# Gates and branches of the second block by token rows, another order of the modulation folds, an earlier start of the [hi|lo] products in the first feed-forward

## The chip, the cores and the metric

The kernel runs on one core of a Trainium2 chip. The metric is the device time of one execution in microseconds (us). Three runs of the kernel before took 802.23, 802.59 and 802.83 us, so the median is 802.59 us. The profile comes from one further execution, which took 802.78 us.

## The reference

The input is 256 tokens (S) of 1024 channels (D). Two transformer blocks follow each other; all numbers are float32.

- Block one: `mod = silu(c) @ w_ada + b_ada` gives six vectors of 1024: shift1, scale1, gate1, shift2, scale2, gate2. `h = rmsnorm(x) * (1 + scale1) + shift1`, `proj = h @ w_in`; a sliding-window attention and a differential attention; `merged = sigmoid(ga) * (out_a @ w_branch_swa) + sigmoid(gd) * (out_d @ w_branch_diff)`; `x = x + gate1 * (merged @ w_out)`; then `x = x + gate2 * conv_ffn(rmsnorm(x) * (1 + scale2) + shift2)`, a feed-forward of width 2816 with a causal convolution of width 3 and a GELU gate.
- Block two: `proj = rmsnorm(x) @ w_in_2` gives a short convolution, a block attention (moba), a cross attention to a memory, and three gates g1, g2, g3 of 1024 channels each. `merged = sigmoid(g1 + bg1) * (y_conv @ w_br_conv) + sigmoid(g2 + bg2) * (y_moba @ w_br_moba) + sigmoid(g3 + bg3) * (y_mem @ w_br_mem)`; `x = x + merged @ w_o`; then a feed-forward with SiLU.

The sigmoid is computed as `0.5 * (1 + tanh(z / 2))`; the factor 0.5 is applied when the merged sum is rounded.

## The kernel before, in words

**Products in two parts.** Every float32 operand is split into a rounded high part (`whi`, `hhi`) and the rest (`wlo`, `hlo`). A product is three matmuls: hi by hi, hi by lo, lo by hi. `hhi` and `hlo` are the halves of one tile, `h_two`.

**Units.** The weights arrive as 131 units of 128 x 2048 numbers (1 MB), in a ring of four raw slots (`raw`). SyncE loads a unit, ScalarE (ACT) rounds it (`round_unit`, line 516), VectorE (DVE) subtracts to get the low part (`split_low`, line 1100), TensorE (PE) multiplies. ACT and DVE work three units ahead (`AHEAD`). The order of the loads is the list `PLAN` (`build_plan`, line 50). Units are named by the first of their stage: `WIN1` (block one's input projection), `BR1` (4 units of branches), `WO1` (4 units of output projection), `FFN1` (33 units), then `WIN2` (26 units, the last 12 are the gates), `BR2` (6), `WO2` (4), `FFN2` (33).

**Four shapes of a unit's products.** (a) By channels (`channels`, `both_channels`, `abreast_half`): the weights are stationary, 256 token columns move, 48 matmuls of 256 columns. (b) Paired (`paired_channels`, `paired_half`): the high weights are stationary and `[hi|lo]` of the input move together as 512 columns, then the low weights with 256 columns: 16 matmuls of 512 and 16 of 256. The two halves of the PSUM bank have to be added afterwards: ACT copies one half out, DVE adds the other. (c) By token rows (`tall`, `branch_rows`): the input is stationary, 512 weight columns move, 24 matmuls of 512 columns; the result has tokens on the partitions. (d) Wide: the first four units of the first feed-forward (`wide_up`), whose moving operand has 256 tokens and two columns with the shift (`wide_hi`, `wide_lo`, 258 columns).

**Folds of the modulation.** `w_ada` is 24 pieces of 1 MB, each with the weights of two tiles of `mod`. `fold_ada` (line 1066) multiplies a piece with the spread silu(c) and sums it: two DVE instructions for a piece. From piece 10 on the pieces share the ring with the weights; `after` in `build_plan` says behind which unit a piece comes, and `split_low` of that unit is followed on DVE by the fold (`fold_after`). Pieces 12 to 15 make shift2, 16 to 19 scale2, 20 to 23 gate2.

**From block one's merge to its feed-forward.** DVE and ACT work in program order. In block one the merge is by rows (`merge`, k == 0, into `x_rows`); PE turns the merged rows to channels by eight 128 x 128 transposes for each half (`turn_merged`, line 2160), ACT rounds them, DVE makes the low part. Then DVE: gains, `shift_out` (a copy of shift2), the two shift columns of `wide_lo` (line 1450), and for u = 0 to 3 the new x of two channel tiles (line 1469), the low part of the scaled x (line 1174), the sums of squares (line 1122) and, at u = 1 and 2, `split_low` of units FFN1 and FFN1+1. PE starts `wide_up` when `wide_lo_ready` is set, takes channel tile after tile as `glo_ready` counts up, and after tile 5 sums the squares (`statistics("two")`, line 1889), which needs the squares of all eight tiles.

**Block two before.** Its gate units are paired: ACT copies the low half, DVE adds (line 1621), ACT takes the tanh with the bias as a scalar per channel. Its branches are by channels (`branch`), merged straight in channel layout (`mg`), so there is nothing to turn.

Of the kernel before, what the change touches and what calls it, by code (L numbers as in the profile page):

```python
# [18 lines left out]
ALU = mybir.AluOpType  # L19
# [119 lines left out]
MERGED_BANK = (2, 0)  # L139
# [3 lines left out]
FIRST_PAIRED = (4, 2)  # L143
PAIRED_A, PAIRED_G = ((0, 1), (0, 1)), ((2, 3), (2, 3))
# [7 lines left out]
def ring_landings(entry):  # L152
# [6 lines left out]
        WIN2: (0, 1), WIN2 + 2: (2, 7), WIN2 + 4: (0, 1), WIN2 + 6: (2, 7)}  # L159
# [7 lines left out]
def is_paired(w):  # L167
    return PAIRED_IN2 <= w < BR2


def unit_banks(w):
# [9 lines left out]
    for first, b in ((WO1, 4), (WO2, 6)):  # L181
        if first <= w < first + 4:
            return ((b + w - first) % 8,)
# [5 lines left out]
def build_evacuations():  # L189
# [7 lines left out]
    for w in [*range(FFN1), *range(WIN2, FFN2)]:  # L197
        if w == WIN2:
            last_in = {}
        if is_paired(w):  # L200
# [5 lines left out]
            if kind == "cc":  # L206
                done[w] = done[w, 1]
            else:
                emptied_by("act" if kind == "g" else "dve", w)
            continue  # L210
        on_dve = BR1 <= w < FFN1 or BR2 <= w < FFN2
# [26 lines left out]
def two_blocks(nc, t, out):  # L238
    ctx = ExitStack()
    with ctx:  # L240
# [52 lines left out]
        gate, _ = place("gate", [P, 24, S], F32, at=scratch_at)  # L293
        gate_rows, _ = place("gate_rows", [P, 2, NT, D], F32, at=scratch_at)
# [24 lines left out]
        def low_tile(k, i):  # L319
            kind = IN2[k][0]  # L320
            if kind == "g":
                return gate[:, 2 * (k - 14) + i, :]
# [4 lines left out]
        A_LOW = ("low_copied", "a_low1")  # L327

# [16 lines left out]
        half_bg = small[:, 64:88]  # L345
# [50 lines left out]
        def _(sp):  # L396
# [8 lines left out]

            def load_beside(a):
# [15 lines left out]
            for r, (kind, n) in enumerate(PLAN):  # L422
                if r == 3:
                    sp.dma_start(vec[:, FIRST_VECTORS:NV], t["vectors"][:, FIRST_VECTORS:NV]).then_inc(sem("vec_landed"), 16)
                if (kind, n) == ("ada", 4):
                    sp.dma_start(lam_in[:, :, :].rearrange("p a b -> p (a b)"), t["diff_lambda"])\
                        .then_inc(sem("lam_landed"), 16)
                if r == 2:
                    sp.dma_start(xt[:, :, :], t["x_rows"].rearrange("(a p) b -> p a b", p=P)).then_inc(sem("xt_landed"), 16)
                if (kind, n) == ("w", WIN1 + 13):  # L430
                    sp.dma_start(x[:, :, :].rearrange("p a b -> p (a b)"), t["x"]).then_inc(sem("x_landed"), 16)
                if (kind, n) == ("w", WIN1 + 9):
                    sp.wait_ge(sem("hlo_ready"), KT)
                    sp.dma_start(memt[:, :, :], t["mem_rows"].rearrange("(a p) b -> p a b", p=P))\
                        .then_inc(sem("memt_landed"), 16)
# [78 lines left out]
        def _(act):  # L514
# [230 lines left out]
            for s in range(18):  # L745
# [43 lines left out]
                if s == 13:  # L789
                    act.wait_ge(sem("memt_landed"), 16)  # L790
# [26 lines left out]
            def merge_and_project(b0, nbr, o0, k, name, gain):  # L817

                for u in range(1, 2 * nbr):
                    if k and u == nbr:  # L820
                        round_merged(k, 0)
                    if u < 2 * nbr - 1:
                        round_unit(b0 + u + AHEAD)
                if k == 0:
                    round_turned(0)
                    round_unit(o0 + AHEAD - 1)
                    round_turned(1)
                else:
                    round_merged(k, 1)
                    round_unit(o0 + AHEAD - 1)  # L830
                for u in range(4):
# [3 lines left out]
                    if k == 0 and u == 0:  # L835
# [12 lines left out]
            def round_turned(half):  # L848
                act.wait_ge(sem("turned_in"), 3 + half)
                for i in range(2):  # L850
                    c = 4 * half + 2 * i
                    copy(hhi[:, c:c + 2, :], pair(ps[:, MERGED_BANK[half] + i, :]), scale=0.5).then_inc(sem("mghi_ready"), 1)

            def round_merged(k, half):
                for i in range(2):
                    act.wait_ge(sem("merged"), 4 * k + 2 * half + i + 1)
                    c = 4 * half + 2 * i
                    copy(hhi[:, c:c + 2, :], mg[:, c:c + 2, :], scale=0.5).then_inc(sem("mghi_ready"), 1)
# [7 lines left out]
            def ffn(f):  # L866
# [45 lines left out]
                def slot(c, kind, j, it=0):  # L912
# [18 lines left out]
                    if f == 1 and c == 2:  # L931
                        act.wait_ge(sem("turned_in"), 7)
# [34 lines left out]
            for s in range(27):  # L967
                if s == 2:
                    root("memk", tokens=eps_mem)
                if s >= 1:  # L970
# [23 lines left out]
                    else:  # L994
# [42 lines left out]
        def _(dve):  # L1037
# [191 lines left out]
            V.tensor_scalar(half_bg, col("b_gate_2", n=24), 0.5, None, ALU.mult)  # L1229
# [24 lines left out]
            dve.wait_ge(sem("lam_landed"), 16)  # L1254
# [129 lines left out]
            def merge(w, b, nbr, k, by_bank=False):  # L1384
# [3 lines left out]
                for i, bank in enumerate(unit_banks(w)):  # L1388
                    if by_bank and i == 1:
                        dve.wait_ge(gemm_done, w + 1)  # L1390
                    c = 4 * half + 2 * i
                    if k == 0:
                        g = gate_rows[:, r, i, 512 * half:512 * half + 512]
                        dst, sums, term = x_rows[:, i, 512 * half:512 * half + 512], ps[:, bank, :], probs[:, i, 0:512]
                    else:
                        g = gate[:, KT * r + c:KT * r + c + 2, :]
                        dst, sums, term = mg[:, c:c + 2, :], pair(ps[:, bank, :]), pair(probs[:, i, 0:512])
# [18 lines left out]
            def low_merged(k, half):  # L1416
                for i in range(2):
                    dve.wait_ge(sem("mghi_ready"), 4 * k + 2 * half + i + 1)
                    c = slice(4 * half + 2 * i, 4 * half + 2 * i + 2)
                    src = mg[:, c, :] if k else pair(ps[:, MERGED_BANK[half] + i, :])  # L1420
                    V.scalar_tensor_tensor(out=hlo[:, c, :], in0=src, scalar=0.5, in1=f32(hhi[:, c, :]),
                                           op0=ALU.mult, op1=ALU.subtract).then_inc(sem("mglo_ready"), 1)

            def merge_all(b0, nbr, o0, k):
                for u in range(1, 2 * nbr):
                    merge(b0 + u - 1, u - 1, nbr, k)
                    if k and u % nbr == 0:
                        low_merged(k, 0)
                    if u < 2 * nbr - 1:
                        split_low(b0 + u + AHEAD)  # L1430
                if k == 0:
                    low_merged(k, 0)
                merge(b0 + 2 * nbr - 1, 2 * nbr - 1, nbr, k, by_bank=True)
                if k == 0:
                    split_low(o0 + AHEAD - 1)
                    low_merged(k, 1)
                else:
                    low_merged(k, 1)
                    split_low(o0 + AHEAD - 1)
# [3 lines left out]
            def two_gain(c):  # L1443
# [8 lines left out]
            dve.wait_ge(sem("x_landed"), 16)  # L1452
            dve.wait_ge(raw_done, ada_folded(2))
            for u in range(4):
# [167 lines left out]

            def mix_norm():
# [16 lines left out]
            for s in range(27):  # L1640
# [112 lines left out]
        def _(pe):  # L1753
# [379 lines left out]
            def branch(w, tile0, waits, last=False):  # L2133
                begin(w)
                for s_, n in waits:
                    pe.wait_ge(s_, n)
                for i in range(4):
# [278 lines left out]
```

## Time and profile before

| | us |
|---|---|
| median of three runs | 802.59 |
| the profiled execution | 802.78 |
| its span, first to last instruction | 801.0 |
| PE busy | 791.0 (99%) |
| DVE busy | 638.2 (80%) |
| ACT busy | 454.3 (57%) |
| POOL busy | 32.1 (4%) |

The span is 1.8 us shorter than the execution. PE's granted clock was 1.00 over the whole span. A busy PE is modelled: a matmul's shown duration overlaps with the next one's, so the pace of PE is read from the distance of the starts, not from the durations.

### The profile page before, as it was taken

The numbers are of one execution on the slowest core, as the hardware profiler recorded it, in microseconds if no ns is written. First come the engines' busy times: TensorE is split into PE (matmuls) and PEld (weight loads), VectorE is DVE, ScalarE is ACT, GpSimd is POOL, SyncE is SP. The second block draws the span as 40 slices with busy tenths as digits, with TensorE's granted clock in tenths as the row PEclk, the third lists the DMA queues.
The fourth block names the chain that finished last, engine by engine and source line by source line (L and its number), as shares of the span: only waits on it lengthen the run. The fifth ranks groups of instructions, "written<-read, shape, count | busy, mean of one in ns | idle before, by whom it ended". The sixth has DMA issues, their size and how long they took to land.

```text
span 801.0 us, 12246 instructions
## 1 busy us (share of the span) xinstructions
PE 791.0 (99%) x4888; PEld 704.6 (88%) x4888; DVE 638.2 (80%) x955; ACT 454.3 (57%) x649; POOL 32.1 (4%) x32
## 2 busy tenths in 40 slices
PE   7999999999999999999999999999999999999998
PEld 7899778889999888888888888889999988888887
DVE  4998999997888987776887898755777777777775
ACT  7848677637556345454876657775436644545451
POOL 2000000000000000000000000000000121111210
DMA  9996948964536866554354544444444555455411
GB/s 359 420 420 248 355 165 304 381 253 158 215 137 236 317 254 215 203 209 160 136 185 160 203 158 158 158 158 158 158 169 153 210 209 207 158 209 212 170 41 53
DMA packets 25480, 168.86 MB, mean 211 GB/s; under 512 B 2896, under 2 KB 3408, under 8 KB 5840
## 3 DMA queue, kind: packets, MB, share of 16 engines
q1 hardware_dynamic: 25280, 168.08, 56.7%
q8 instruction: 39, 0.64, 0.3%
q14 instruction: 17, 0.14, 0.1%
q10 hardware_dynamic: 144, 0.01, 0.0%
HBM read 167.03 MB, written 1.05 MB: 210 GB/s over the span
## 4 chain that ended last, share of the span: by engine, by line
PE 88%; DVE 7%; DMA 2%; ACT 2%; issue 1%; SPq 0%; ACTq 0%
PE ps L1761 46%; PE ps L1796 23%; PE ps L1803 12%; DVE wlo L1100 2%; PE ps L1857 2%; DVE raw L1066 1%; PE ps L2037 1%; DMA raw<-in_w_mem_kv 1%; ACT whi L516 1%; PE ps L2070 1%; PE ps L2008 1%; PE ps L2009 1%; DMA raw<-in_branches 1%; DVE wlo L1095 1%; DVE side_x L1066 0%
## 5 line engine op out<-in xcount | busy, mean ns | idle before, releaser
L1100 DVE TENSOR_TENSOR wlo<-raw,whi 128x2048 fp32r<-128x2048 f32 (+1 forms) x130 | 287.1, 2215 | 62.6 <-ACT whi L516 58.3
L516 ACT ACTIVATE whi<-raw 128x2048 fp32r<-128x2048 f32 (+2 forms) x144 | 251.0, 1756 | 82.2 <-PE ps L1796 42.6
L1796 PE MATMUL ps<-h_two,whi 128*128 128x512 f32 x512 | 123.8, 392 | 0.0
L1796 PEld LDWEIGHTS ps<-h_two,whi 128*128 128x128 f32 x512 | 94.1, 188 | 18.3
L1761 PE MATMUL ps<-h_two,whi 128*128 128x256 f32 x544 | 99.3, 285 | 1.8 <-DVE wlo L1095 1.6
L1761 PEld LDWEIGHTS ps<-h_two,whi 128*128 128x128 f32 x544 | 84.7, 192 | 2.8 <-DVE wlo L1095 1.8
L1761 PE MATMUL ps<-h_two,wlo 128*128 128x256 f32 x272 | 76.9, 283 | 0.0
L1761 PE MATMUL ps<-whi,fhi 128*128 128x512 f32 (+1 forms) x178 | 69.1, 388 | 0.0
L1761 PE MATMUL ps<-whi,flo 128*128 128x512 f32 (+1 forms) x178 | 68.9, 387 | 0.0
L1761 PE MATMUL ps<-wlo,fhi 128*128 128x512 f32 (+1 forms) x178 | 68.8, 387 | 0.0
L1796 PE MATMUL ps<-g_two,whi 128*128 128x512 f32 x288 | 68.4, 390 | 0.0
L1803 PEld LDWEIGHTS ps<-h_two,wlo 128*128 128x128 f32 x512 | 65.4, 191 | 3.5 <-issue 1.0
L1803 PE MATMUL ps<-h_two,wlo 128*128 128x256 f32 x512 | 67.6, 285 | 0.0
L1796 PEld LDWEIGHTS ps<-g_two,whi 128*128 128x128 f32 x288 | 53.5, 188 | 10.7
L499 POOL TENSOR_TENSOR fg<-fg,spread_r 128x512 f32<-128x512 f32 x11 | 27.3, 2480 | 743.1 <-ACT fg L516 743.1
L516 ACT ACTIVATE fhi<-fp 128x512 fp32r<-128x512 f32 x22 | 13.9, 632 | 68.7 <-DVE fp L1567 50.1
L1761 PEld LDWEIGHTS ps<-h_two,wlo 128*128 128x128 f32 x272 | 52.1, 192 | 0.0
L1761 PE MATMUL ps<-whi,h_two 128*128 128x512 f32 x160 | 50.2, 395 | 0.0
L1761 PE MATMUL ps<-whi,g_two 128*128 128x512 f32 x128 | 40.1, 395 | 0.0
L1761 PEld LDWEIGHTS ps<-whi,fhi 128*128 128x128 f32 x178 | 33.4, 188 | 7.1 <-issue 0.4
L1761 PEld LDWEIGHTS ps<-wlo,fhi 128*128 128x128 f32 x178 | 33.4, 188 | 6.8
L1761 PEld LDWEIGHTS ps<-whi,flo 128*128 128x128 f32 x178 | 33.4, 188 | 6.6
(278 smaller groups left out, 1424.1 us busy)
## 6 DMA issues: line engine op xcount, KB each, us to landing
raw<-in_w_up SPq DMA_DIRECT2D x44, 1024.0 KB, 4.8
raw<-in_w_in SPq DMA_DIRECT2D x43, 1024.0 KB, 4.8
raw<-in_w_down SPq DMA_DIRECT2D x22, 1024.0 KB, 4.8
raw<-in_w_ada SPq DMA_DIRECT2D x14, 1024.0 KB, 5.2
raw<-in_branches SPq DMA_DIRECT2D x10, 1024.0 KB, 4.8
raw<-in_w_out SPq DMA_DIRECT2D x4, 1024.0 KB, 6.9
raw<-in_w_o SPq DMA_DIRECT2D x4, 1024.0 KB, 4.7
raw<-in_w_mem_kv SPq DMA_DIRECT2D x3, 1024.0 KB, 11.2
```

Of the source, the lines that this page charges most:

```text
L499: nc.gpsimd.tensor_tensor(fg[:, b, :].rearrange("p (a b) -> p a b", a=2), fg[:, b, :].rearrange("p (a b) -> p a b", a=2), spread_r[:, :].u ...
L516: return nc.scalar.activation(dst, src, func, **kw)
L1066: ins = V.tensor_tensor_reduce(out=piece, in0=piece, in1=cs[:, :], scale=1.0, scalar=col("b_ada", c), op0=ALU.mult, op1=ALU.add, accum_out ...
L1095: V.tensor_tensor(wlo[:, w % SPLIT, 0:c], raw[:, slot, 0:c], f32(whi[:, w % SPLIT, 0:c]), ALU.subtract).then_inc(sem("half_lo"), 1)
L1100: V.tensor_tensor(wlo[:, w % SPLIT, c:UNIT], raw[:, slot, c:UNIT], f32(whi[:, w % SPLIT, c:UNIT]), ALU.subtract).then_inc(raw_done, 1)
L1761: ins = mm(out_, l, r, start=start and i == 0, stop=stop and i == 2, **kw)
L1796: ins = mm(ps[:, b, :], wt(whi, w, kt, P * i, P, 256), two[:, :, kt, :], start=start and kt == 0, stop=stop and kt == KT - 1, skip_group_c ...
L1803: ins = mm(ps[:, b, S:2 * S], wt(wlo, w, kt, P * i, P, 256), two[:, 0, kt, :], start=start and kt == 0, stop=stop and kt == KT - 1, skip_g ...
L1857: ins = mm(ps[:, b, S * i:S * i + S], wt(w_, w, kt, P * i, P, 256), a_[:, kt, :], start=kt == 0 and i == 0 and n == 0, stop=kt == KT - 1 a ...
L2008: mm(ps[:, b, 0:first], q[:, 0:P], k[:, 0:first], start=True, stop=True)
L2009: ins = mm(ps[:, b, first:first + 256], q[:, P:2 * P], k[:, 0:256], start=True, stop=True)
L2037: ins = nc.tensor.transpose(ps[:, b, dst:dst + P], probs[:, m, src:src + P], ident[:, :])
```

## The change

1. The 12 gate units of block two go by rows, two units sharing two PSUM banks. The gate bias comes as rows: three loads of 1 MB (`load_bias`) into the gate tile, DVE adds PSUM to it (`add_bias`, two instructions of 128 x 512 for two units), ACT takes the tanh (two of 128 x 512). The copies of low halves go, and the small `half_bg`.
2. The six branch units of block two go by rows (`branch_rows`), merged in rows, turned by `turn_merged(1, 0)` and `(1, 1)`, and the first two units of `WO2` are taken half by half as in block one. Unit `WO2+2` is paired and its result added in two steps.
3. The folds: pieces 16 to 19 come before 12 to 14, nothing stands behind `BR1+3`, piece 15 comes behind unit `FFN1`, pieces 20 to 23 behind `FFN1+15, 18, 21, 24`. `shift_out` is copied at u = 1, `wide_lo`'s shift columns are made at u = 2 of the loop over `WO1`.
4. The first feed-forward's products are paired from column pair 3 on, before from 4 (two units). The bank pairs change parity.

```diff
-    after = {WIN1 + at: (a,) for a, at in enumerate((9, 12, 13, 14, 15, 16, 17, 18, 19, 20), 10)}
-    after[WIN1 + 10] = (9,)
-    after.update({FFN1 + at: (a,) for a, at in enumerate((9, 12, 15, 18), 20)})
+    behind = {9: 10, 10: 9, 12: 11, 13: 16, 14: 17, 15: 18, 16: 19, 17: 12, 18: 13, 19: 14, FFN1 - WIN1: 15}
+    after = {WIN1 + at: (a,) for at, a in behind.items()}
+    after.update({FFN1 + at: (a,) for a, at in enumerate((15, 18, 21, 24), 20)})
...
-MERGED_BANK = (2, 0)
+MERGED_BANK = ((2, 0), (6, 4))
+PAIRED_OUT2 = 2
...
-FIRST_PAIRED = (4, 2)
-PAIRED_A, PAIRED_G = ((0, 1), (0, 1)), ((2, 3), (2, 3))
+FIRST_PAIRED = (3, 2)
+PAIRED_A, PAIRED_G = ((2, 3), (0, 1)), ((0, 1), (2, 3))
...
+        **{WIN2 + 14 + 2 * p: ((2, 6), (0, 1))[p % 2] for p in range(6)}}
...
+                if (kind, n) == ("w", WIN2 + 15):
+                    sp.wait_ge(sem("x3_ready"), 1)
+                    load_bias(0)
+                if (kind, n) == ("w", WIN2 + 23):
+                    sp.wait_ge(sem("yclo_ready"), 2)
+                    load_bias(1)
+                    load_bias(2)
...
             def gate_tanh(k):
-                if k < 0 or IN2[k][0] != "g":
+                if k < 14 or k % 2 == 0:
                     return
-                w, g = WIN2 + k, 2 * (k - 14)
-                for i in range(2):
-                    act.wait_ge(emptied["dve"], EVACUATED[w, i][1])
-                    ins = copy(gate[:, g + i, :], gate[:, g + i, :], ACT.Tanh, scale=0.5, bias=half_bg[:, g + i:g + i + 1])
-                ins.then_inc(emptied["act"], 1)
+                r, columns = gate_pair(k)
+                for tt in range(NT):
+                    act.wait_ge(emptied["dve"], EVACUATED[WIN2 + k - 1 + tt][1])
+                    g = gate_rows[:, r, tt, columns]
+                    copy(g, g, ACT.Tanh, scale=0.5)
...
-            dve.wait_ge(raw_done, ada_folded(3))
-            V.tensor_copy(shift_out, mod[:, 24:32]).then_inc(sem("shift_ready"), 1)
-            dve.wait_ge(sem("wide_hi_ready"), 1)
-            V.tensor_tensor(wide_lo[:, :, S:WIDE], mod[:, 24:32].unsqueeze(2).to_broadcast([P, KT, 2]),
-                            f32(wide_hi[:, :, S:WIDE]), ALU.subtract).then_inc(sem("wide_lo_ready"), 1)
...
                 if u in (1, 2):
                     sum_squares("two", SQUARES["two"], mg, u - 1)
                     split_low(w + AHEAD)
+                if u == 1:
+                    dve.wait_ge(raw_done, ada_folded(3))
+                    V.tensor_copy(shift_out, mod[:, 24:32]).then_inc(sem("shift_ready"), 1)
+                if u == 2:
+                    dve.wait_ge(sem("wide_hi_ready"), 1)
+                    V.tensor_tensor(wide_lo[:, :, S:WIDE], mod[:, 24:32].unsqueeze(2).to_broadcast([P, KT, 2]),
+                                    f32(wide_hi[:, :, S:WIDE]), ALU.subtract).then_inc(sem("wide_lo_ready"), 1)
...
+            def add_bias(k):
+                r, columns = gate_pair(k)
+                dve.wait_ge(gemm_done, WIN2 + k + 1)
+                dve.wait_ge(sem(BIAS_LANDED[r]), 32)
+                for tt in range(NT):
+                    g = gate_rows[:, r, tt, columns]
+                    V.tensor_tensor(g, g, ps[:, unit_banks(WIN2 + k)[tt], :], ALU.add).then_inc(emptied["dve"], 1)
...
+                xs, banks = x[:, 2 * u:2 * u + 2, :], unit_banks(w)
+                if u == PAIRED_OUT2:
+                    link(V.tensor_tensor(xs, xs, half_of(banks, 0), ALU.add))
+                sums = half_of(banks, 1) if u == PAIRED_OUT2 else pair(ps[:, banks[0], :])
+                V.tensor_tensor(xs, xs, sums, ALU.add).then_inc(sem("x5_ready"), 1)
...
             def project_merged(o0, k):
-                if k == 0:
-                    begin(o0)
-                    ...
+                begin(o0)
+                abreast_half(o0, k, 0, 0)
+                turn_merged(k, 1)
+                begin(o0 + 1)
+                abreast_half(o0, k, 1, 0)
+                for u in range(2):
+                    abreast_half(o0, k, u, 1)
+                for u in (2, 3):
                     begin(o0 + u)
-                    if u == 0:
-                        both_channels(o0, (sem("mglo_ready"), 4 * k, 2))
+                    if k and u == PAIRED_OUT2:
+                        paired_channels(o0 + u, unit_banks(o0 + u), h_two, False)
                         continue
...
-                branch(BR2 + u, 4 * r, [[(sem("yclo_ready"), 2)], [(sem("ylo_ready"), 8)], [(sem("ylo_ready"), 10)]][r], last=u == 5)
+                if u == 4:
+                    turn_merged(1, 0)
+                branch_rows(BR2 + u, 4 * r, [[(sem("yclo_ready"), 2)], [(sem("ylo_ready"), 8)], [(sem("ylo_ready"), 10)]][r], u == 5)
```

## Rows read from the trace of the kernel before

**Rows 1.** The page: busy time, share of the span and instructions of each engine.
```profile
PE 791.0 (99%) x4888; PEld 704.6 (88%) x4888; DVE 638.2 (80%) x955; ACT 454.3 (57%) x649; POOL 32.1 (4%) x32
```
**Rows 2.** Waits of PE: who waited for whom, us in total, times, longest.
```profile
PE ps L1944 <- DVE small L1207: 4.2, 1, 4.2
PE ps L1761 <- DVE wlo L1095: 1.8, 2, 1.6
```
**Rows 3.** Table by stretches: length, busy us of each engine, clock, DMA; BR1, then BR2.
```profile
153.33:176.12 22.79, 22.79 (x106) 18.77 (x104) 21.16 (x26) 9.74 (x8) 0.00 (x0) 1.00 0.88 331
...
555.08:589.63 34.55, 34.55 (x289) 34.55 (x288) 25.62 (x27) 12.71 (x12) 0.00 (x0) 1.00 0.51 183
```
**Rows 4.** Timeline of PE, gate units: start, duration, operation, count.
```profile
542.10 3.82 PE L1796 MATMUL ps<-h_two,whi 128*128 128x512 f32 x16
545.76 2.08 PE L1803 MATMUL ps<-h_two,wlo 128*128 128x256 f32 x16
547.67 3.82 PE L1796 MATMUL ps<-h_two,whi 128*128 128x512 f32 x16
```
**Rows 5.** Timeline of PE: where units start in WO1 and FFN1.
```profile
194.26 0.40 PE L1761 MATMUL ps<-h_two,whi 128*128 128x256 f32 x2
...
200.02 0.28 PE L1761 MATMUL ps<-wide_hi,whi 128*128 128x258 f32 x1
...
204.37 0.95 PE L1889 MATMUL ps<-mean_d,proj 128*128 128x1 f32 x8
...
241.14 0.40 PE L1761 MATMUL ps<-whi,fhi 128*128 128x512 f32 x1
...
246.60 0.40 PE L1761 MATMUL ps<-h_two,whi 128*128 128x256 f32 x2
```
**Rows 6.** The chain that ended last, in order of time: the two turns.
```profile
169.81 0.99 PE ps L2160 x8
...
179.16 0.87 PE ps L2160 x8
```
**Rows 7.** Timeline of DVE during WO1.
```profile
188.71 0.88 DVE L1469 SCALAR_TENSOR_TENSOR x<-ps,small,x 128x256 f32<-128x256 f32 x2
...
192.14 2.29 DVE L1100 TENSOR_TENSOR wlo<-raw,whi 128x2048 fp32r<-128x2048 f32 x1
194.47 0.88 DVE L1469 SCALAR_TENSOR_TENSOR x<-ps,small,x 128x256 f32<-128x256 f32 x2
...
197.64 2.29 DVE L1100 TENSOR_TENSOR wlo<-raw,whi 128x2048 fp32r<-128x2048 f32 x1
199.85 0.48 DVE L1469 SCALAR_TENSOR_TENSOR x<-ps,small,x 128x256 f32<-128x256 f32 x1
```
**Rows 8.** Timeline of DVE: a fold's first instruction and what follows the fold.
```profile
160.99 1.28 DVE L1066 CUSTOM_DVE_ANT_0 raw<-raw,cs,vec 128x1024 f32<-128x1024 f32 x1
...
163.40 1.28 DVE L1399 SCALAR_TENSOR_TENSOR x_rows<-gate_rows,ps 128x512 f32<-128x512 f32 x2
```
**Rows 9.** Timeline of DVE during WO1: `wide_lo`'s shift columns, then the first x.
```profile
185.84 0.18 DVE L1450 TENSOR_TENSOR wide_lo<-small,wide_hi 128x16 fp32r<-128x16 f32 x1 [0.28 <-ACT wide_hi L516]
186.31 0.88 DVE L1469 SCALAR_TENSOR_TENSOR x<-ps,small,x 128x256 f32<-128x256 f32 x2 [0.29 <-issue]
```
**Rows 10.** Timeline of ACT: the square of tile 7.
```profile
203.49 0.40 ACT L516 ACTIVATE proj<-x 128x256 f32<-128x256 f32 x1
```
**Rows 11.** Timeline of DVE: the product of pair 2 in the first feed-forward.
```profile
252.83 0.68 DVE L1569 TENSOR_TENSOR fp<-fg,ps 128x512 f32<-128x512 f32 x1
```
**Rows 12.** The gate tile: count, duration in ns min/median/max, first and last start.
```profile
L1621 DVE TENSOR_TENSOR gate<-gate,ps x24: 410/414/422, 483.7 to 556.0; 128x256 f32<-128x256 f32 x24
```
**Rows 13.** Timeline of DVE in BR2 and WO2: first of a merge, then an x.
```profile
572.55 0.69 DVE L1403 SCALAR_TENSOR_TENSOR probs<-gate,ps 128x512 f32<-128x512 f32 x1 [0.57 <-PE ps L1761]
...
612.94 0.69 DVE L1724 TENSOR_TENSOR x<-x,ps 128x512 f32<-128x512 f32 x1 [0.62 <-PE ps L1761]
```
**Rows 14.** The page: DMA issues, KB each, median us from issue to landing.
```profile
raw<-in_w_in SPq DMA_DIRECT2D x43, 1024.0 KB, 4.8
```

More of the change, by code:

```diff
@@ L167, in is_paired @@
 def is_paired(w):
-    return PAIRED_IN2 <= w < BR2
+    return PAIRED_IN2 <= w < WIN2 + 14
 def unit_banks(w):
@@ L180, in unit_banks @@
             return (b, b + 1)
-    for first, b in ((WO1, 4), (WO2, 6)):
-        if first <= w < first + 4:
-            return ((b + w - first) % 8,)
+    if WO1 <= w < WO1 + 4:
+        return (4 + w - WO1,)
+    if WO2 <= w < WO2 + 4:
+        return ((6,), (7,), (0, 1), (3,))[w - WO2]
     if w >= WIN1 + FIRST and w < WIN2:
@@ L208, in build_evacuations @@
             else:
-                emptied_by("act" if kind == "g" else "dve", w)
+                emptied_by("dve", w)
             continue
-        on_dve = BR1 <= w < FFN1 or BR2 <= w < FFN2
+        on_dve = BR1 <= w < FFN1 or WIN2 + 14 <= w < FFN2
         emptied_by("x1" if WO1 <= w < FFN1 else "x5" if WO2 <= w < FFN2 else "dve" if on_dve else "act", w)
@@ L292, in two_blocks @@
         side_proj, _ = place("side_proj", [P, 2, D], F32, at=proj_at + 8 * S * 4)
-        gate, _ = place("gate", [P, 24, S], F32, at=scratch_at)
-        gate_rows, _ = place("gate_rows", [P, 2, NT, D], F32, at=scratch_at)
+        gate_rows, _ = place("gate_rows", [P, 3, NT, D], F32, at=scratch_at)
         tmp, _ = place("tmp", [P, KT, S], F32, at=scratch_at + 16 * S * 4)
@@ L819, in merge_and_project @@
                 for u in range(1, 2 * nbr):
-                    if k and u == nbr:
-                        round_merged(k, 0)
                     if u < 2 * nbr - 1:
                         round_unit(b0 + u + AHEAD)
-                if k == 0:
[L825 to L830, printed above, removed]
+                round_turned(k, 0)
+                round_unit(o0 + AHEAD - 1)
+                round_turned(k, 1)
                 for u in range(4):
@@ L846, in merge_and_project, with round_turned @@
                         square(x, mg, u, sem(name))
-            def round_turned(half):
-                act.wait_ge(sem("turned_in"), 3 + half)
+            def round_turned(k, half):
+                act.wait_ge(sem("turned_in"), (3, 7)[k] + half)
                 for i in range(2):
                     c = 4 * half + 2 * i
[L852 to L858, printed above, removed]
+                    copy(hhi[:, c:c + 2, :], pair(ps[:, MERGED_BANK[k][half] + i, :]), scale=0.5).then_inc(sem("mghi_ready"), 1)
             merge_and_project(BR1, 2, WO1, 0, "x1_ready", lambda c: gs2[:, c:c + 1])
@@ L1390, in merge @@
                         dve.wait_ge(gemm_done, w + 1)
[L1391 to L1397, printed above, removed]
+                    g = gate_rows[:, r, i, 512 * half:512 * half + 512]
+                    dst, sums, term = x_rows[:, i, 512 * half:512 * half + 512], ps[:, bank, :], probs[:, i, 0:512]
                     if r == 0:
@@ L1419, in low_merged @@
                     c = slice(4 * half + 2 * i, 4 * half + 2 * i + 2)
-                    src = mg[:, c, :] if k else pair(ps[:, MERGED_BANK[half] + i, :])
-                    V.scalar_tensor_tensor(out=hlo[:, c, :], in0=src, scalar=0.5, in1=f32(hhi[:, c, :]),
+                    V.scalar_tensor_tensor(out=hlo[:, c, :], in0=pair(ps[:, MERGED_BANK[k][half] + i, :]), scalar=0.5, in1=f32(hhi[:, c, :]),
                                            op0=ALU.mult, op1=ALU.subtract).then_inc(sem("mglo_ready"), 1)
@@ L1426, in merge_all @@
                     merge(b0 + u - 1, u - 1, nbr, k)
-                    if k and u % nbr == 0:
-                        low_merged(k, 0)
                     if u < 2 * nbr - 1:
                         split_low(b0 + u + AHEAD)
-                if k == 0:
-                    low_merged(k, 0)
+                low_merged(k, 0)
                 merge(b0 + 2 * nbr - 1, 2 * nbr - 1, nbr, k, by_bank=True)
[L1434 to L1439, printed above, removed]
+                split_low(o0 + AHEAD - 1)
+                low_merged(k, 1)
                 split_low(o0 + AHEAD)
@@ L1646, in _ @@
                     add_halves(s - 1)
+                if s > 14 and s % 2 == 0:
+                    add_bias(s - 1)
                 if s not in ITEMS2:
@@ L2131, in _ @@
                 slot(w, ITEMS1, s, halves)
[L2133 to L2137, printed above, removed]
-                    channels(w, i, 512, yhi[:, tile0:tile0 + 4, :], ylo[:, tile0:tile0 + 4, :], 4, last=i == 3,
-                             signal=sem("first_bank_done") if last and i == 1 else None)
             def branch_rows(w, tile0, waits, last):
```

56 lines of the change are left out of this document (25 added, 31 removed), and 2 rows, old and new, of the table VECTORS.

## The prediction

> **What bounds the kernel now.** I read the page's first part, PE's own list of waits, the table by stretches and the timeline of PE. PE is busy 99% of the span and DVE 80% [rows 1]. PE waits only in the start-up: 4.2 us for the spread of c and 1.8 us for a low part [rows 2]; none of its waits from 50 us on, but for a few tenths in block one's attention, is in that list. The reader is to see a stream of matmuls without holes, so the time is the number of matmuls by their pace, and the pace is the distance of starts. Whatever leaves this stream is gained in full, and whatever holds PE in a place where it was never held is lost in full. So there are two sums: the pace of the forms that change, and a look at each place where DVE or ACT works differently, asking whether PE comes to wait. The clock is 1.00 in both stretches of [rows 3], so a nanosecond is the same all along.
>
> **Paces.** By channels (48 matmuls of 256): 194.26 to 200.02, 5.76 us a unit [rows 5]; BR2's six units give the same, 34.55 / 6 = 5.76 [rows 3]. Paired: 542.10 to 547.67, 5.57 us [rows 4]. By rows (24 of 512): BR1's four units and one turn take 22.79 us [rows 3], the turn 0.99 [rows 6], so (22.79 - 0.99) / 4 = 5.45 us; the down unit from 241.14 to 246.60, the same shape, took 5.46 [rows 5].
>
> **Part 1, gate units by rows.** 12 x (5.57 - 5.45) = 1.4 us off PE. DVE's work shrinks: before, 24 adds of 414 ns [rows 12], after, 12 of about 0.69 (the 128 x 512 add from PSUM, [rows 13]), so 9.9 becomes 8.3 us; ACT loses 24 copies and keeps as many tanh columns. Only even steps have `add_bias`, and attention items sit on odd ones, so the attention's chain gets shorter. A bank pair comes back two units after `add_bias` was due, over 5 us of cover. The bias loads are 3 MB more on SP's queue. Two waits of SP precede them: `x3_ready` and `yclo_ready`; both are set by DVE in the step whose `split_low` releases the neighbouring weight load anyway, and what is queued behind (a unit needed three steps, some 16 us, later) takes 4.8 us to land [rows 14]. I count them at nothing; if the three transfers went strictly one behind another it would be 3 x 4.8 = 14.4 us, still under 16. Bounds 0 to 2 us, taken 0.
>
> **Part 2, branches by rows.** 34.55 - 6 x 5.45 = 1.85 us off PE. `WO2+2` paired: 5.76 - 5.57 = 0.2 off. Two turns are added, priced by block one's, 0.99 and 0.87 [rows 6]: 1.86 us on. Do PE's new waits bite? A merge is four operations of 0.69 [rows 13], 2.9 us with what lies between them, a split 2.3 [rows 7]; together 5.2 in a unit that shrinks from 5.76 to 5.45. Before, DVE still waited 0.57 us for PE ahead of a merge [rows 13], so about 0.25 is left. The turn of half 0 comes one whole unit after its merge is due, the turn of half 1 a half unit (2.9 us) after the last matmul of BR2, against 0.2 + two operations (1.4) for the last merge. Block one does exactly this, there with folds between [rows 8], and its turns cost 0.99 and 0.87 and no wait [rows 2, 6]. I take no wait; bounds 0 to 1 us. The paired `WO2+2` costs DVE one more add (0.7), which ends in the 0.62 us that DVE waited before the last x [rows 13]; PE needs what follows only for its tile 6, over 4 us into FFN2. Nothing.
>
> The trace prices the forms at 5.76 and 5.45 [rows 3]. The Trainium skill ("TensorE: Matmul & The Clock Gate", Back-to-back issue gap) has, for a single matmul, N/2.4 + 2.5 ns, so 109 ns at 256 and 216 at 512: by it a unit is 5.24 by channels and 5.18 by rows, and parts 1, 2 and 4 would bring 0.7 us of PE together in place of 3.8; the sum would end 3.1 us higher. The rows time this very pair of forms, so the measurement decides. The same page (Part 4: PE-mode transpose) has about 275 ns for a transpose in a kernel; 16 of them would be 4.4 us, while the rows have 1.86, since here they follow each other closer than their durations.
>
> **Part 4, pair 3 of the first feed-forward.** Two units, 2 x (5.76 - 5.57) = 0.4 off. The new condition is that g(3) starts only when product 2 is done, before product 1 was enough. Product 2 was ready at 253.5 [rows 11], and g(3) will want to start at 246.60 + 5.57 = 252.2 [rows 5]: it would be 1.3 late, but the fold that stood in that step (2.4 us, below) moves to a later one, so 251.1. Nothing; 1.3 us if I am wrong on that.
>
> **Part 3, the folds.** A fold is 163.40 - 160.99 = 2.41 us of DVE [rows 8]. Taken from `BR1+3`, where PE was not waiting for DVE, it brings PE nothing. It is put behind `split_low(FFN1)`, in the u = 1 step of WO1, and DVE runs in order. Here is the loop before [rows 7]: u = 1 from 188.71, split of FFN1 from 192.14, x of u = 2 at 194.47, split from 197.64, x of tile 6 at 199.85. The inserted: 2.41 fold, about 0.25 for its wait and the copy of shift2. Off it come 0.1 of DVE slack before 194.47 and about 0.4, since the copy and the shift columns that delayed the first x to 186.31 [rows 9] are gone and ACT's rounding starts as much earlier. Net +2.15: x of u = 2 at 196.6, the second split ends at 199.85 + 2.15 = 202.0, and only then come the shift columns (0.18), so `wide_lo_ready` at 202.2. PE wants it at 200.02 [rows 5]. **PE waits 2.2 us** where it never did. A second chain through the same delay: PE sums the squares 4.35 us into the unit (204.37 - 200.02), and the square of tile 7 ended at 203.9 [rows 5, 10]; it moves by 2.3 to 206.2, PE's place to 202.2 + 4.35 = 206.55. The two overlap, and only the first is paid. If DVE's cover is better than I think, the wait is 0; if worse, 2.6. Taken 2.2.
>
> The fold's later place in the feed-forward (pieces 20 to 23) falls in steps of the same make as those which held one before; nothing. `half_bg` leaves the start-up, 0.1 at most.
>
> **The sum.** Off: 1.4 + 1.85 + 0.2 + 0.4 + 0.1 = 3.95. On: 1.86 + 2.2 = 4.06. Net +0.1 us: 801.0 + 0.1 of span plus 1.8 outside is 802.9 against the profiled 802.78. The median shown is 0.2 below that execution, so I forecast 802.7. A measurement of this kernel tells 0.2%, 1.6 us, from no change; this is the same.
>
> **Rivals.**
> - *The fold is covered.* PE does not wait at FFN1: 802.7 - 2.2 = 800.5, faster by 0.26%. For it: DVE was only 80% busy, and it loses a fold before WO1 [rows 1, 8]. Against: in WO1 it idled only 0.1 us between the split of 192.14 and the next x, and one wait inside an in-order queue can't be caught up from before. Chance 0.19.
> - *Both waits of the first wide unit add (slower).* PE waits for the shift columns, and then for the squares at its tile 6, because ACT, which now sits in its u = 2 step behind `shift_ready`, passes the delay on a second time. It decides from the point where tile 7's square comes more than 4.35 us after PE's start; if it came late by the whole chain again, 2.3 more: 805.0, slower by 0.3%. Against: my 206.2 stands before 206.55, if by 0.35 only, and before the change the same chain was ready at 203.9 for 204.37. With a late turn in block two (1 us) instead, the time is 803.7, which is still the same. Chance 0.08.
> - *The bias or the banks arrive late.* DVE stands in `add_bias`, splits behind it are late and PE waits; 2 us, 804.7. A unit's cover of 16 us speaks against. Chance 0.03.
> - *Rows bring no pace in block two.* The change does not do what it says: 1.4 + 1.85 missing, 806.0. Against: [rows 3] of block one. Chance 0.02.
>
> **Numbers.** Forecast 0.68. Faster 0.21: the covered case, and 0.02 of the forecast's for a half-covered wait that passes 801.0. Slower (above 804.2) 0.13, the three last rivals. Same 0.66. The likeliest case's own range is 802.0 to 803.7 (wait of 1.8 to 2.6, turns up to 1 late). The range for 8 in 10 takes in the covered case: 800.4 to 803.9.
>
> **What would show it.** Right: in the timeline of PE a hole of about 2 us ahead of the first matmul of 258 columns, released by DVE's line for the shift columns of `wide_lo`; two folding instructions between a split and an x in DVE's WO1; gate and branch units 5.45 us apart; two turns of eight transposes in block two at 0.9 each with no idle time; DVE's list with 12 adds on the gate rows. Wrong: no hole there and everything else as said gives 800.5; a hole in front of the turns, of `WO2`, of g(3) or at the sums of squares gives more than 802.7.

## The result, and the profile after

The kernel before takes 802.65 us (802.23 to 803.87, 12 runs), the changed one 804.18 us (802.82 to 806.03, 12 runs): a ratio of 1.0018, 95% interval 1.001 to 1.0026. I forecast 802.7 and a range up to 803.9, so the time is outside. The profiled execution of the changed kernel took 804.81 us, with a span of 802.7 and a mean granted clock (the share of TensorE's full speed) of 0.998; that of before 802.78, 801.0 and 1.000.

The page's first part after, for [rows 1]. PE is busy 1.5 us less, the half clock told of below included, and DVE as long as before:
```profile
PE 789.5 (98%) x4616; PEld 691.5 (86%) x4616; DVE 639.0 (80%) x945; ACT 446.1 (56%) x614; POOL 32.1 (4%) x32
```
PE's waits after, for [rows 2]: who waited for whom, us in total, times, longest.
```profile
PE ps L1948 <- DVE small L1209: 4.4, 1, 4.4
PE ps L1765 <- DVE wlo L1097: 3.0, 3, 1.6
PE ps L1765 <- DVE wlo L1102: 2.0, 1, 2.0
PE ps L1960 <- DVE wlo L1219: 0.7, 2, 0.5
```
The third is new, one wait of 2.0 us; the others lie in the start-up, as in [rows 2]. The timeline of DVE in WO1 shows where it comes from, against [rows 7, 9]:
```profile
191.83 2.29 DVE L1102 TENSOR_TENSOR wlo<-raw,whi 128x2048 fp32r<-128x2048 f32 x1
194.04 1.28 DVE L1068 CUSTOM_DVE_ANT_0 raw<-raw,cs,vec 128x1024 f32<-128x1024 f32 x1
...
195.24 1.28 DVE L1068 CUSTOM_DVE_ANT_0 raw<-raw,cs,vec 128x1024 f32<-128x1024 f32 x1
...
196.57 0.17 DVE L1466 COPY small<-small 128x8 f32<-128x8 f32 x1
196.65 0.87 DVE L1452 SCALAR_TENSOR_TENSOR x<-ps,small,x 128x256 f32<-128x256 f32 x2
...
199.81 2.29 DVE L1102 TENSOR_TENSOR wlo<-raw,whi 128x2048 fp32r<-128x2048 f32 x1
202.02 0.17 DVE L1469 TENSOR_TENSOR wide_lo<-small,wide_hi 128x16 fp32r<-128x16 f32 x1
```
The fold stands between the split of FFN1's weights and the x of u = 2; everything behind it is 2.2 us later, and the shift columns of `wide_lo` are the last of it. The timeline of PE over the same place is the one to read line by line; the first number is the start, so the distance from line to line is the pace:
```profile
199.96 0.28 PE L1765 MATMUL ps<-h_two,wlo 128*128 128x256 f32 x1
202.29 0.36 PE L1765 MATMUL ps<-wide_hi,whi 128*128 128x258 f32 x1 [2.05 <-DVE wlo L1102]
202.48 0.28 PE L1765 MATMUL ps<-wide_lo,whi 128*128 128x258 f32 x1
202.60 0.28 PE L1765 MATMUL ps<-wide_hi,wlo 128*128 128x258 f32 x1
202.72 0.28 PE L1765 MATMUL ps<-wide_hi,whi 128*128 128x258 f32 x1
202.84 0.35 PE L1765 MATMUL ps<-wide_lo,whi 128*128 128x258 f32 x1
202.99 0.42 PE L1765 MATMUL ps<-wide_hi,wlo 128*128 128x258 f32 x1
203.21 0.42 PE L1765 MATMUL ps<-wide_hi,whi 128*128 128x258 f32 x1
203.42 0.42 PE L1765 MATMUL ps<-wide_lo,whi 128*128 128x258 f32 x1
...
206.22 0.34 PE L1765 MATMUL ps<-wide_hi,wlo 128*128 128x258 f32 x1
206.39 0.28 PE L1765 MATMUL ps<-wide_hi,whi 128*128 128x258 f32 x1
206.51 0.29 PE L1765 MATMUL ps<-wide_lo,whi 128*128 128x258 f32 x1
...
208.21 0.95 PE L1893 MATMUL ps<-mean_d,proj 128*128 128x1 f32 x8
```
The hole is where the prediction put it: PE starts at 202.29 instead of 200.02 [rows 5]. What follows wasn't in the prediction. The first matmuls behind the hole come 0.12 us apart, then, from 202.99 on, the same ones come 0.215 apart, until 206.2. The table by stretches says why (length; busy us of PE, PEld, DVE, ACT and POOL; granted clock; DMA share; GB/s):
```profile
199.00:203.00 4.00, 1.95 (x17) 1.78 (x16) 3.51 (x5) 2.17 (x2) 0.00 (x0) 0.99 0.42 176
203.00:206.20 3.20, 3.20 (x17) 3.20 (x16) 2.40 (x6) 1.30 (x5) 0.00 (x0) 0.50 0.89 325
206.20:208.00 1.80, 1.80 (x17) 1.80 (x16) 0.16 (x1) 1.75 (x1) 0.00 (x0) 0.97 0.01 5
```
The granted clock is 0.50 for 3.2 us, the lower of the two levels, 1.2 GHz. PE had been at work at 1.00, since 50 us with waits of a few tenths at most, then it was idle for 2.2 us, then back at work for 0.6 us at 1.00 before the clock fell. The price by the starts: 18 distances from 202.84 to 206.51 are 3.67 us, and at 0.12 would be 2.16, so 1.5 us. PE counts as busy all along: neither the list of waits nor the busy share shows this loss, only the clock column and the distance of starts do.

Block two, from the timeline of DVE:
```profile
568.32 0.69 DVE L1399 SCALAR_TENSOR_TENSOR probs<-gate_rows,ps 128x512 f32<-128x512 f32 x1 [1.14 <-PE ps L1765]
...
573.76 0.69 DVE L1399 SCALAR_TENSOR_TENSOR probs<-gate_rows,ps 128x512 f32<-128x512 f32 x1 [0.25 <-PE ps L1765]
...
579.20 1.28 DVE L1395 SCALAR_TENSOR_TENSOR x_rows<-gate_rows,ps 128x512 f32<-128x512 f32 x2 [0.25 <-PE ps L1765]
```
Each line follows the end of a branch unit: they are 5.44 us apart, against 5.76 by channels [rows 3, 5], and DVE waits 0.25 us for PE, the slack that the prediction left it. The chain that ended last, in block two, has the turns:
```profile
569.86 9.30 PE ps L1765 x41
579.16 0.87 PE ps L2156 x8
580.03 13.77 PE ps L1765 x72
593.80 0.87 PE ps L2156 x8
```
and the gate tile's list (count, duration in ns min/median/max, first and last start) has 12 adds where [rows 12] had 24:
```profile
L1620 DVE TENSOR_TENSOR gate_rows<-gate_rows,ps x12: 672/680/687, 493.8 to 558.0; 128x512 f32<-128x512 f32 x12
```

### The profile page after: what moved, and what is told of

Same layout as the page of the kernel before. It is cut to its first block, busy times and chain, and to the rows that moved or that the text cites. A ratio compares the mean times of both kernels' runs of the same rounds, so it can differ in the third digit from the quotient of the medians.

```text
span 802.7 us, 11659 instructions
## 1 busy us (share of the span) xinstructions
PE 789.5 (98%) x4616; PEld 691.5 (86%) x4616; DVE 639.0 (80%) x945; ACT 446.1 (56%) x614; POOL 32.1 (4%) x32
## 4 chain that ended last, share of the span: by engine, by line
PE 90%; DVE 6%; ACT 2%; DMA 1%; issue 1%; SPq 0%; DVEq 0%; ACTq 0%
PE ps L1765 54%; PE ps L1800 19%; PE ps L1807 10%; DVE wlo L1102 2%; PE ps L1861 1%; PE ps L2041 1%; DMA raw<-in_w_mem_kv 1%; PE ps L2074 1%; ACT whi L530 1%; PE ps L2012 1%; PE ps L2013 1%; DVE wlo L1097 1%; DVE raw L1068 1%; DVE side_x L1068 0%; PE ps L2156 0%
## 5 line engine op out<-in xcount | busy, mean ns | idle before, releaser
L1765 PE MATMUL ps<-whi,h_two 128*128 128x512 f32 x352 | 110.7, 396 | 0.0
L1765 PE MATMUL ps<-h_two,whi 128*128 128x256 f32 x480 | 87.9, 285 | 1.7 <-DVE wlo L1097 1.6
L1800 PE MATMUL ps<-h_two,whi 128*128 128x512 f32 x368 | 88.0, 390 | 0.0
L1800 PEld LDWEIGHTS ps<-h_two,whi 128*128 128x128 f32 x368 | 68.0, 188 | 13.5
L1765 PEld LDWEIGHTS ps<-h_two,whi 128*128 128x128 f32 x480 | 74.7, 191 | 2.7 <-DVE wlo L1097 1.8
L1765 PEld LDWEIGHTS ps<-whi,h_two 128*128 128x128 f32 x352 | 64.9, 188 | 13.3 <-issue 0.7
L1765 PE MATMUL ps<-wlo,h_two 128*128 128x512 f32 x176 | 68.7, 390 | 0.0
L1765 PE MATMUL ps<-h_two,wlo 128*128 128x256 f32 x240 | 67.8, 283 | 0.0
L1807 PEld LDWEIGHTS ps<-h_two,wlo 128*128 128x128 f32 x368 | 46.3, 191 | 1.8 <-issue 0.7
L1807 PE MATMUL ps<-h_two,wlo 128*128 128x256 f32 x368 | 47.2, 283 | 0.0
L1765 PEld LDWEIGHTS ps<-h_two,wlo 128*128 128x128 f32 x240 | 46.0, 191 | 0.0
L1765 PE MATMUL ps<-whi,yhi 128*128 128x512 f32 (+1 forms) x112 | 40.5, 362 | 0.7 <-DVE wlo L1097 0.7
L1765 PE MATMUL ps<-wlo,yhi 128*128 128x512 f32 (+1 forms) x112 | 40.2, 359 | 0.0
```

Of the source, the lines that this page charges most:

```text
L1765: ins = mm(out_, l, r, start=start and i == 0, stop=stop and i == 2, **kw)
L1800: ins = mm(ps[:, b, :], wt(whi, w, kt, P * i, P, 256), two[:, :, kt, :], start=start and kt == 0, stop=stop and kt == KT - 1, skip_group_c ...
L1807: ins = mm(ps[:, b, S:2 * S], wt(wlo, w, kt, P * i, P, 256), two[:, 0, kt, :], start=start and kt == 0, stop=stop and kt == KT - 1, skip_g ...
```

## The experiments

**The fold and its companions put back.** Everything of the change stays but Part 3's hold on WO1:
```
-    behind = {..., 19: 14, FFN1 - WIN1: 15}
+    behind = {..., 19: 14, 20: 15}
```
with the copy of shift2, the shift columns of `wide_lo` and ACT's rounding of them ahead of the WO1 loop again.

> The changed kernel with piece 15 behind BR1+3 again (not behind FFN1), and the shift copy and the shift columns of wide_lo ahead of the loop over WO1 again. Rows, turns, pair 3, the order of the other pieces and the later pieces 20 to 23 stay. Theory A (the wait at the first wide unit costs its 2.2 us, and 1.65 us more because the granted clock is halved for 3.3 us after it): no hole before the first matmul of 258 columns, clock 1.00 throughout, 804.2 - 3.85 = 800.3 us. Theory B (the wait costs only its length; the remaining 1.5 us over the forecast come from the bias loads, the turns or the new rows): 804.2 - 2.2 = 802.0 us. Theory C (nothing of it is in part 3): 804.2 us.

Measured: 800.67 us (800.28 to 801.24, 11 runs) against 802.62 for before; 0.9975, interval 0.9967 to 0.9984. The clock is 1.000 in all 11. There is no hole at FFN1, as the timeline of PE shows:
```profile
199.75 0.28 PE L1763 MATMUL ps<-h_two,wlo 128*128 128x256 f32 x1
199.87 0.28 PE L1763 MATMUL ps<-wide_hi,whi 128*128 128x258 f32 x1
200.00 0.28 PE L1763 MATMUL ps<-wide_lo,whi 128*128 128x258 f32 x1
```
Parts 1, 2 and 4 bring 1.95 us together. It is faster than both kernels, by 0.25% than before; the next version is within 0.05 us of it. In the span they bring 2.2 us (798.6 against 800.8, medians), and the time outside the span takes 0.2 back: its median is 1.95 to 2.05 us in every version with the rows of block two, and 1.8 in before, in Part 3 alone and in pair 3 alone.

**Only the fold put back**, the copy and the shift columns in their new steps:

> The changed kernel with only piece 15 put back behind BR1+3; the shift copy stays at u = 1 and the shift columns at u = 2. Theory A: the inserted fold is the cause; the second split of the loop ends at 199.8 again, the columns at 200.0 to 200.1, so PE waits 0.1 to 0.3 us and the clock stays: 800.3 to 800.7 us. Rival: the columns' place behind the second split is what holds PE, by about 2 us, and lowers the clock: 804 us.

Measured: 800.72 us (800.24 to 801.37, 11 runs), 0.9978 (0.997 to 0.9987), all at clock 1.000. In the trace PE's last matmul of WO1 starts at 199.34 and its first wide one at 199.55, 0.1 us later than the pace of 0.12 would have it. So the later place of the small operations costs nothing that shows in the time; the 2.4 us of fold in that step is what makes the hole.

**Part 3 alone**, on the kernel before:
```
...
-    after[WIN1 + 10] = (9,)
...
+    behind = {9: 10, 10: 9, ..., 19: 14, FFN1 - WIN1: 15}
...
```
with pieces 20 to 23 and the fold's companions moved as in the change.

> The kernel before with part 3 alone: the new order of the pieces, piece 15 behind FFN1, 20 to 23 later, the shift steps at u = 1 and u = 2. No rows in block two, no pair 3. Theory A: a hole of 2.2 us at 200.0 and a clock drop behind it, 802.65 + 3.85 = 806.5 us. Theory B: 804.9 us. Theory C: 802.7 us.

Measured: 804.76 us (804.43 to 805.4, 8 runs), 1.0028 (1.0018 to 1.0039). The hole is there, but all eight executions have clock 1.000, and the cost is 804.76 - 802.62 = 2.14 us, the hole's length and no more. What I expected with the clock's fall, 806.5, didn't come, so with this run alone the clock was in doubt.

**The changed kernel again**, on another chip:

> The changed kernel once more, beside the two that hold PE, on one chip. Refined theory A: PE's hole of 2.2 us is in every execution, the halved clock behind it only in some (9 of 12 before). Executions whose mean clock is 1.00 take about 802.9 us, those at 0.998 about 804.2; the median depends on how many fall. Rival: the time over the forecast is in executions of either clock alike.

Measured: 803.05 us (802.35 to 804.41, 11 runs), 1.0009 (1.0 to 1.0018). Here 4 executions have a clock of 0.998 and take 803.92 to 804.41; the seven at 1.000 have a median of 802.79. The profiled one was of the latter. Its stretches at FFN1:
```profile
199.00:202.00 3.00, 0.95 (x9) 0.78 (x8) 2.96 (x4) 1.38 (x1) 0.00 (x0) 1.00 0.42 178
202.00:204.00 2.00, 2.00 (x17) 2.00 (x18) 1.39 (x4) 0.82 (x2) 0.00 (x0) 1.00 0.57 156
204.00:206.00 2.00, 2.00 (x19) 2.00 (x18) 1.34 (x4) 1.07 (x3) 0.00 (x0) 1.00 0.87 369
```
PE is busy 0.95 of the 3.00 us from 199, so the hole is the same, and no half clock follows it. So the same program has it in some executions and not in others.

**The shift columns one step earlier**, the fold left where the change has it:
```
-                if u == 2:
+                if u == 1:
                     dve.wait_ge(sem("wide_hi_ready"), 1)
```

> The changed kernel with the fold where it is, but DVE makes the shift columns of wide_lo at u = 1, right behind the copy of shift2. Theory A with its second chain: PE starts the first wide unit at 200.0, and then waits about 2 us at its sums of squares, which need tile 7's square at about 206.5 where PE comes by at 204.4; the hole has moved, its size and what follows it not: 803.5 to 804.7 us. Rival (the shift columns alone held PE): 800.3 to 801 us.

Measured: 803.87 us (802.65 to 806.76, 12 runs), 1.0017 (1.0007 to 1.0027). PE's first wide matmul no longer waits (200.73, then 200.85), and the delay comes out at the sums of the squares:
```profile
206.10 0.61 PE L1893 MATMUL ps<-mean_d,proj 128*128 128x1 f32 x4 [0.75 <-DVE proj L1124]
207.34 0.61 PE L1893 MATMUL ps<-mean_d,proj 128*128 128x1 f32 x4 [0.63 <-ACT proj L530]
```
From the first wide matmul to the transposes of `rstd` it is 209.49 - 200.85 = 8.64 us, against 206.54 - 199.87 = 6.67 with the fold put back: 2.0 us, the same price in another place. That is the second chain of the prediction: it overlapped with the first, and once the first wait was gone it was paid instead. Moving the needed columns out of the fold's way doesn't help; the delay sits in DVE's queue and reaches PE by the next edge. The profiled execution took 803.76 us; about 1 us of that is older than the hole (its first wide matmul starts at 200.85 against 199.87, behind longer waits in the start-up), while the median of the five executions at clock 1.000 is 802.75, again 800.7 and 2.1. The other seven fell: four have a clock of 0.998 (median 804.10) and three 0.996 (805.18). So in this version, whose wait comes in two pieces of 0.75 and 0.63 us, executions fell as well; none of the fallen was profiled, so where in them the clock was low isn't shown.

**A hole without any change of DVE's order.** On the version with everything put back, GpSimd clears a spare 128 x 512 tile when WO1's matmuls are done, and PE waits for it before the first wide matmul, on a count of a semaphore that exists:
```
...
+            pool.wait_ge(gemm_done, FFN1)
+            for i in range(3):
+                nc.gpsimd.memset(spare[:, :], 0.0).then_inc(sem("const_made"), 1)
+                pool.wait_ge(sem("const_made"), MADE_ALL + i + 1)
...
                     pe.wait_ge(sem("wide_lo_ready"), 1)
+                    if c == 0:
+                        pe.wait_ge(sem("const_made"), MADE_ALL + 3)
```

> The kernel with fold and code back (800.67 us), and PE alone held ahead of the first matmul of 258 columns: GpSimd clears a spare tile three times once WO1 is done, and PE waits for that. DVE and ACT keep their work and order. Theory A: a hole of 2 to 2.4 us costs its length in every execution, 802.9, and where the clock falls behind it 1.3 to 1.7 more, to 804.4; if the hole by itself is what lowers the clock, some executions show 0.998. Rival (the clock falls only with the fold of the changed kernel on DVE): all executions at 1.00 and 802.9 us.

Measured: 803.96 us (802.19 to 805.26, 11 runs), 1.0013 (1.0004 to 1.0022). Four executions at clock 1.000 have a median of 802.69, which is 800.67 and the hole of 2.03; seven at 0.998 have 804.38. The profiled one is of these: the three clears on POOL, then PE's first wide matmul, then the stretches:
```profile
200.04 1.69 POOL L521 MEMSET spare<- 128x512 f32 x3 [181.33 <-PE ps L1768]
201.95 0.36 PE L1768 MATMUL ps<-wide_hi,whi 128*128 128x258 f32 x1 [2.03 <-DVE wide_lo L1181]
...
202.00:204.00 2.00, 2.00 (x11) 2.00 (x12) 1.26 (x3) 1.19 (x3) 0.00 (x0) 0.61 0.88 369
204.00:206.00 2.00, 2.00 (x12) 2.00 (x11) 0.00 (x0) 1.43 (x1) 0.00 (x0) 0.54 0.00 0
206.00:208.00 2.00, 2.00 (x19) 2.00 (x19) 0.00 (x0) 0.00 (x0) 0.00 (x0) 1.00 0.00 0
```
The profile puts PE's wait down to DVE's L1181, but that instruction had ended at 201.12; the last clear ended at 201.73, 0.2 us before PE's start. An idle PE, with DVE's order as in the version without a hole, is enough to bring the half clock in some executions.

**The same with six clears:**

> The same with six clears: a hole of 4 to 4.4 us. Theory A: a longer hole lowers the clock in more executions, or for longer: all below 1.00, 800.7 + 4.2 + 1.6 or more = 806.5 us and above. Rival (clock falls by chance and not by the hole): 804.9 us at 1.00 in most.

Measured: 807.15 us (806.37 to 807.78, 5 runs), 1.0054 (1.004 to 1.0068); all five below 1.000, four at 0.996. PE stands still from 200.1 to 204.04, and the stretches are:
```profile
202.00:204.00 2.00, 0.00 (x0) 0.00 (x0) 1.39 (x4) 0.85 (x3) 1.66 (x4) 0.79 1.01 422
204.00:206.00 2.00, 1.96 (x9) 1.99 (x10) 0.18 (x1) 1.77 (x1) 0.00 (x0) 0.50 0.02 8
206.00:208.00 2.00, 2.00 (x11) 2.00 (x11) 0.00 (x0) 0.00 (x0) 0.00 (x0) 0.50 0.00 0
208.00:210.00 2.00, 2.00 (x12) 2.00 (x11) 0.00 (x0) 0.00 (x0) 0.00 (x0) 0.50 0.00 0
210.00:212.00 2.00, 2.00 (x19) 2.00 (x19) 0.00 (x0) 0.00 (x0) 0.00 (x0) 1.00 0.00 0
```
Here the clock falls while PE still stands (0.79 in the first line), stays low for 6 us of matmuls and costs about 2.7: 807.15 less 800.67 and the hole of 3.8.

**Pair 3 alone**, on the kernel before, with the folds where they were:
```
-FIRST_PAIRED = (4, 2)
+FIRST_PAIRED = (3, 2)
```
and the bank pairs swapped as in the change.

> The kernel before with pair 3 of the first feed-forward paired and the banks' parity changed, the folds where they were. The forecast said that g(3) would then wait 1.3 us for product 2 (253.5 against 252.2), and that the later folds are what spares it. If so: PE's list shows about 1.3 us on DVE's line of fp, and the time is 802.6 - 0.4 + 1.3 = 803.5 us. Rival: product 2 is in time even with the fold; no such wait, 802.2 us.

Measured, in a single execution: 804.9 us, at a clock of 1.000. g(3) waits, in the timeline of PE:
```profile
254.69 0.59 PE L1803 MATMUL ps<-h_two,wlo 128*128 128x256 f32 x3 [1.38 <-DVE fp L1569]
```
That is the 1.3 us which the prediction spared because a fold leaves that step. The time is 1.4 us over the expected 803.5, and PE's list of waits has most of that:
```profile
PE ps L2113 <- DVE proj L1374: 1.3, 1, 1.3
```
This wait stands at 148 us, in block one's differential attention, far ahead of the edit and of FFN1; PE's first wide matmul comes 1.0 us later than before (201.03 against 200.02). Why this execution has it stays open: with one execution, whether it belongs to the edit can't be told.

**Part 3 alone and the changed kernel, side by side.** After the runs above, only the kernel of Part 3 alone had a hole of 2 us and never a half clock.

> The kernel before with the fold of piece 15 moved (and with it the wide_lo columns) and nothing else, a second time, beside the changed kernel on one chip. Theory A, the fall of the granted clock behind the 2 us hole is a matter of chance from execution to execution and of the chip: here some executions at clock 0.998 near 806.2 (804.6 + 1.65), the rest near 804.7, and the share is like that of the changed kernel beside it. Theory B, with block two's parts as before the clock does not fall behind this hole: all executions at 1.000 and 804.4 to 805.4, while the changed kernel beside it shows some at 0.998.

> The changed kernel a third time, beside folds_only_again. Executions at clock 1.000 near 802.9 and at 0.998 near 804.2. By theory A their shares are those of folds_only_again on the same chip, whatever they are; by theory B only this one has executions at 0.998.

Measured: Part 3 alone 805.8 us (804.87 to 806.94, 5 runs), 1.0044 (1.0031 to 1.0057), four of five at 0.998; the changed kernel 802.95 us (802.41 to 805.64, 12 runs), 1.001 (1.0001 to 1.0018), three of twelve at 0.998. Theory B falls: the kernel that never showed the half clock on one chip shows it here in most executions.
```profile
202.00:204.00 2.00, 2.00 (x15) 2.00 (x14) 1.59 (x5) 0.61 (x2) 0.00 (x0) 0.71 0.92 250
204.00:206.00 2.00, 2.00 (x11) 2.00 (x11) 0.96 (x3) 1.49 (x3) 0.00 (x0) 0.50 0.65 274
```
Theory A's second half, that the shares on one chip are alike, is neither confirmed nor refuted: 4 of 5 and 3 of 12 differ, but five executions are few.

## Why the prediction was wrong

**The step that failed** is the price of the wait in Part 3. The prediction puts the hole at its length, "PE waits 2.2 us", under the sentence that the clock is 1.00 in both stretches read, "so a nanosecond is the same all along". Those stretches held no hole, so they could not say that of the time behind one. The missing term is half clock behind the hole, 1.5 us where it comes. Grouped by clock, the three batches of the changed kernel (35 executions) give

| clock of the execution | executions | median, us |
|---|---|---|
| 1.000 | 19 (3, 7, 9) | 802.82 |
| 0.998 | 16 (9, 4, 3) | 804.26 |

The upper row is 0.1 us from my forecast of 802.7; the difference of the rows, 1.44 us, is the term. Two of the 19 lie at 803.96 and 804.41, so at clock 1.000 an execution can be late for another reason; before has such too, up to 804.04. Among the 12 executions of the result, 9 had the half clock. Of the kernels without a hole none of 92 executions with a recorded clock did (70 of before, 22 with the fold put back), although the profiled ones have a wait of 1.6 us in the start-up [rows 2]; of those with a hole of about 2 us in one piece 27 of 59 (the changed kernel 16 of 35, Part 3 alone 4 of 13, GpSimd's hold 7 of 11); with 3.8 us 5 of 5; with two shorter waits, in the run with early shift columns, 7 of 12. In the profiled execution the sum is then 802.78 + 0.1 + 1.5 = 804.4 against 804.81. Of the 0.4 left, 0.3 is outside the span (2.1 against 1.8). The longer start-up waits in PE's list, 3.0 against 1.8 us at one line, hardly reach the path: PE's last matmul of WO1 starts at 199.96, so FFN1 could have begun at 200.08, against 200.02 before.

**What held.**
- *Part 3, the chain.* Forecast and measured: x of u = 2 at 196.6 and 196.65, the second split's end at 202.0 and 202.10, PE's start at 202.2 and 202.29, the end of tile 7's square at 206.2 and 206.14 (205.74 and 0.40 in the timeline of ACT). Part 3 alone costs 2.14 us at clock 1.000.
- *Parts 1, 2 and 4 and the bias.* Forecast -3.95 + 1.86 = -2.1 us, measured -1.95 and -1.90. With Part 3's +2.14 that is +0.2, and the executions at clock 1.000 are 802.82 against 802.6: the parts add. That sum holds a term which the prediction took as unchanged, the time outside the span, 0.2 us longer; in the span the parts bring 2.0 to 2.2 us. The bias loads, the banks and the turns bring no wait to PE's list. They weren't run one by one; that their own terms are right is read from the paces of 5.44 and the turns, and what lengthens the time outside the span wasn't looked for.
- *The turns.* 0.87 and 0.87 in the chain, where 0.99 and 0.87 were taken from [rows 6].
- *g(3).* No wait in after, and 1.38 us without the later folds.

**The rivals.** The covered fold is out: the hole stands in every profile of the changed kernel. Of "both waits of the first wide unit add", with 805.0, the size came near and the mechanism is wrong: the eight sums start at 208.21 in one run of lines, without a wait, and the 1.6 us by which they come later than 202.29 + 4.35 is half clock. The two chains overlap, as the run with early shift columns shows from the other side. The time alone would have spoken for that rival.

The Trainium skill ("TensorE: Matmul & The Clock Gate", Back-to-back issue gap) would have put parts 1, 2 and 4 at 0.7 us of PE in place of 3.8, and so, as an estimate by that page, the version with the fold put back at 802.6 - 2.1 + 3.1 = 803.6. It runs at 800.7, so in this case the rows price the forms; the page itself gives this formula for a single matmul, and not for the stream of a kernel.

**What stays open.** Whether an execution falls isn't explained by the kernel or by the chip alone: Part 3 alone fell in 0 of 8 executions on one chip and in 4 of 5 on another, while the run with early shift columns fell in 7 of 12 on the first. What in the moment of the hole decides it I didn't find, so a forecast can only carry it as a chance. A forecast with that chance at one half would still have had 802.7 and 804.2 as its two likely values.

## What to carry to other kernels

Price a hole in a PE that never waits twice: its length, always, and a spell at half clock behind it, here in about half of the executions at 2 us (27 of 59) and in all five at 3.8 us. Splitting the wait in two doesn't spare it: 7 of 12 fell with waits of 0.75 and 0.63 us. Do not put 2.4 us of DVE work between a split and the next x where the idle time in front of that x is 0.1 us, even if the engine is idle a fifth of the span; ask for the first edge to PE behind it, and for the second, which pays if the first is relieved. When a time is off by an amount that no wait shows, read the granted clock stretch by stretch behind each new hole, and sort the executions by their mean clock before explaining the median.

## What the runs showed of the hardware

- Behind a hole of 2.0 to 2.2 us in a busy PE the mean clock shows a fall in 27 of 59 executions; in the four of them that were profiled the granted clock went to 0.50 (1.2 GHz) for 3.2 to 3.4 us, and in the two profiled at 1.000 it stayed at 1.00. Behind 3.8 us it was low for 6 us of matmuls in the profiled one. Where it fell behind the 2 us, it began 0.5 to 1.5 us after PE was back at work (0.6 and 1.5 in the two profiles of the changed kernel); in the longer hole, before PE was back.
- A mean clock of 0.998 for the whole execution, which looks like nothing, stands for this: half clock for 3.3 us of 803 is a loss of 0.5 x 3.3 / 803 = 0.002.
- At half clock matmuls of 258 columns come 0.215 us apart and at full clock 0.12, a factor of 1.8.
